# 42 products that nothing reads, put between the ranks, the tables and the first gathered rows' transposes

## What is computed

```python
g_logits = (hf @ w_group + b_group).astype(f32)      # 4 groups
_, g_idx = lax.top_k(g_logits, 1)
e_sel = jnp.take_along_axis(e_logits, g_idx[:, :, None], axis=1)[:, 0]
top_v, top_i = lax.top_k(e_sel, TOP_K_INNER)         # 2 of 8 experts
...
for e in range(N_EXPERTS):                           # 32 experts
    ye = (jax.nn.silu(hf @ w_gate[e]) * (hf @ w_up[e])) @ w_down[e]
    y = y + combine[:, e:e + 1] * ye
```

## Time and profile before

| what | value |
|---|---|
| runs | 673.93, 675.0, 675.3 us; median 675.0 us |
| profiled execution | 673.51 us; its span from first to last instruction 671.5 us |
| granted TensorE clock, mean | 0.933 of full speed |
| TensorE (PE) busy | 561.6 us, 84% of the span |
| VectorE, ScalarE, GpSimd busy | 251.1, 191.9, 88.7 us |
| moved by DMA | 166.46 MB, 248 GB/s in the mean |
| chain that ended last, by engine | PE 58%, DMA 23%, DVE 8%, ACT 5%, issue 3% |
| its largest links | weights' landing (`egu<-in_w_gu`) 19%, gate/up (line 2228) 12%, first projections (lines 1734 to 1736) 21% |

### The profile page before, as it was taken

One profiled execution on the slowest core, in us unless ns is written; L12 is line 12 of the kernel. 1 busy time (PEld: TensorE's weight loads), 2 busy tenths in 40 slices (PEclk: granted clock), 3 DMA queues, 4 the chain that ended last, 5 costly groups with the idle time before them and its releaser, 6 DMA issues.

```text
span 671.5 us, 8442 instructions
## 1 busy us (share of the span) xinstructions
PE 561.6 (84%) x3375; PEld 370.9 (55%) x3375; DVE 251.1 (37%) x536; ACT 191.9 (29%) x439; POOL 88.7 (13%) x125
## 2 busy tenths in 40 slices
PE   4999999999989899978999739999968787878720
PEld 4868787777878676665788623434423333333200
DVE  3733355736557356635334941111101111111107
ACT  4440725331334533447343310111101111111110
POOL 5000000011574200002000210121111111110010
PEclk9999999999999899999899859999978888889875
DMA  8120131021235490048698757999999999999339
GB/s 302 50 92 24 63 147 44 37 64 63 95 108 213 174 418 3 1 175 326 229 426 350 268 167 308 417 429 423 422 429 421 425 427 424 425 425 428 159 144 368
DMA packets 24344, 166.46 MB, mean 248 GB/s; under 512 B 4752, under 2 KB 5328, under 8 KB 11120
## 3 DMA queue, kind: packets, MB, share of 16 engines
q1 hardware_dynamic: 17264, 146.36, 54.5%
q0 software_dynamic: 6320, 16.92, 6.5%
q10 hardware_dynamic: 720, 2.62, 1.0%
HBM read 154.74 MB, written 17.43 MB: 256 GB/s over the span
## 4 chain that ended last, share of the span: by engine, by line
PE 58%; DMA 23%; DVE 8%; ACT 5%; issue 3%; POOL 2%; SPq 1%; POOLq 0%; ACTq 0%; DVEq 0%
DMA egu<-in_w_gu 19%; PE twin L2228 12%; PE twin L1734 7%; PE twin L1735 7%; PE twin L1736 7%; PE twin L2248 4%; PE twin L1993 3%; PE twin L1994 3%; PE twin L1995 3%; DMA yg<-ye_dram 2%; DMA X<-in_x 1%; DVE xsT L1669 1%; PE twin L2074 1%; PE twin L1929 1%; POOL zK L663 1%
## 5 line engine op out<-in xcount | busy, mean ns | idle before, releaser
L2228 PE MATMUL twin<-egu,xsT 128*64 128x512 f32 x512 | 128.8, 661 | 40.0 <-DMA egu<-in_w_gu 34.1
L2228 PEld LDWEIGHTS twin<-egu,xsT 128*64 128x64 f32 x512 | 46.1, 151 | 112.6 <-issue 112.6
L1734 PE MATMUL twin<-wH,hH 128*128 128x512 f32 x240 | 97.4, 406 | 0.0
L1735 PE MATMUL twin<-wL,hH 128*128 128x512 f32 x240 | 93.9, 391 | 0.0
L1736 PE MATMUL twin<-wH,hL 128*128 128x512 f32 x240 | 93.8, 391 | 0.0
L1675 DVE TENSOR_TENSOR hs<-sil,twin 128x256 f32<-128x256 f32 x16 | 6.7, 422 | 165.2 <-ACT sil L1062 165.2
L2248 PE MATMUL twin<-edn,hTs 128*64 128x512 f32 x256 | 58.1, 593 | 1.1 <-ACT hTs L1066 1.1
L1062 ACT ACTIVATE sil<-twin 128x256 f32<-128x256 f32 x16 | 6.1, 384 | 168.4 <-PE twin L2228 168.4
L1734 PEld LDWEIGHTS twin<-wH,hH 128*128 128x128 f32 x240 | 45.4, 189 | 10.7 <-issue 1.8
L1736 PEld LDWEIGHTS twin<-wH,hL 128*128 128x128 f32 x240 | 45.2, 188 | 9.9
L1735 PEld LDWEIGHTS twin<-wL,hH 128*128 128x128 f32 x240 | 45.3, 189 | 8.3
(11 more groups left out here) (316 smaller groups left out, 811.7 us busy)
## 6 DMA issues: line engine op xcount, KB each, us to landing
egu<-in_w_gu SPq DMA_DIRECT2D x32, 2048.0 KB, 35.2
edn<-in_w_dn SPq DMA_DIRECT2D x32, 1024.0 KB, 39.3
win<-in_w_main SPq DMA_DIRECT2D x12, 1024.0 KB, 5.1
Kc<-in_cache_kt SPq DMA_DIRECT2D x8, 1024.0 KB, 8.0
Vc<-in_cache_v SPq DMA_DIRECT2D x8, 1024.0 KB, 8.4
X<-in_x SPq DMA_DIRECT2D x10, 512.0 KB, 8.3
yg<-ye_dram SPq DMA_DIRECT2D x5, 1024.0 KB, 8.9
woin<-in_w_out SPq DMA_DIRECT2D x3, 1024.0 KB, 5.4
```

Source lines behind the costliest of these rows:

```text
L1734: pe.matmul(bank[i][:, :], hH[:, d, i, :], wH[k][:, cs], start=(d == 0), stop=False)
L1735: pe.matmul(bank[i][:, :], hH[:, d, i, :], wL[k][:, cs], start=False, stop=False)
L2228: ins = pe.matmul(bank[2 + q][CAP * j:CAP * j + CAP, :], xsT[q][:, c, j * CAP:(j + 1) * CAP], egu[places[j]][:, c, :], start=(c == 0), sto ...
```

## The change

A helper `warm(n)` issues n products of the identity with itself on TensorE, into the first 128 columns of bank 2, with no wait and no semaphore. Ten stand between the first tables and the second ranks, ten between the second ranks and the second tables, and 22 between the second tables and the first transposes of gathered rows. Nothing reads their results; nothing is taken away or moved.

```diff
             router(4)
+            def warm(n):
+
+                for j in range(n):
+                    pe.matmul(bank[2][:, 0:P], ident[:, :], ident[:, :], start=True, stop=True)
+
             tables(0, 0, LATE[0], 1)
+            warm(10)
             ranks(2)
+            warm(10)
             tables(0, *LATE, 2)
+            warm(22)
 
             def xs_tr(r, p, q, half_p):
```

## The result

The changed kernel takes 669.51 us in the median of 20 runs (666.70 to 674.56), the kernel before 673.52 us in the median of 20 (669.04 to 676.63). The ratio is 0.9952, 95% interval 0.9934 to 0.9970: 3.2 us faster, at least 2.0 and at most 4.4. A second measurement gave 670.42 against 672.51 us and 0.9957 (0.9932 to 0.9982). One execution of the kernel before, measured beside the first four experiments, took 1370.32 us and is left out of their ratios.

A forecast was written before the change was run, and what follows sets the result against it. The prediction took the weight stream, started by the first `gu_done`, to bound the kernel. Half clock cost 1.85 + 0.88 = 2.73 us, less 0.05 us of delay; 675.0 - 2.7 = 672.3 us, range 670.9 to 674.4.

The forecast's parts named there:

- What bounds the kernel: The last 200 us are one unbroken weight stream, whose start waits for the first pair's `gu_done` at 409.68 us.
- The fear that a `gu_done` ahead of it gains nothing: At expert 5's load, taken to end at 406.8 us: any gain over 3.0 us would be lost behind it.
- Price of a product: Each added fp32 product is two TensorE instructions, at 0.1155 us each at full clock and 0.213 us at half.
- When the clock comes back: On TensorE, full clock returns 3.8 us after dense work begins at half clock, with bounds 2.6 and 6.1 us.
- the first ten: Products between first tables and second ranks: start at 383.7 us, end at 387.75, making `place` 0.45 us late.
- my upper bound: Full clock returns only after 6.1 us, so the products before the second ranks run wholly at half clock, 1.0 us late.
- Behind them: After the 22: transposes 1.97 to 1.09 us, first gate/up 8.94 to 7.09, so `gu_done` at 407.0 us.
- the sum: For the profiled execution, an earlier `gu_done` moves the weight stream and the end by 2.7 us, to 670.8 us.
- I carry the step over: The 2.7 us gain of the profiled execution is taken off the median of 675.0 us, giving 672.3 us.
- The clock did come back on identity products: Rival: TensorE stays at half clock on these products, `gu_done` is 5.7 us late, 680.7 us; chance 0.06.
- It did not fall again before gate/up: Rival: the clock drops between the products' end and the first gate/up, only 0.9 us gained, 674.1 us; chance 0.11.
- The end moved with the hole: Rival: the DMA hole closes but something else holds the stream, so the end stays at 675.0 us; chance 0.06.

The follow-up runs named there:

- the first four experiments: Changed kernel without its 22 products, without both tens, with transposes for products, with 44 for 22: ratios to before 0.9993, 0.9961, 0.9970, 1.0014.
- the doubled 22: Changed kernel with 44 products in place of the last 22: 673.42 us, ratio to before 1.0014.
- with 13 at the end: Changed kernel plus 13 products before the last pair's gate/up, in the wait for its weights: 668.58 us, ratio to before 0.9952.
- both together: Changed kernel plus 8 products in short waits before the first tables and 13 before the last gate/up: 667.61 us, repeated 668.16 us.

## Why the prediction was right and wrong

*What bounds the kernel* was right. From the first `gu_done` to the last landing it is 217.1 to 217.8 us in twelve of fourteen profiles, whether `gu_done` came at 403 or at 410 us, and the doubled 22 moved the last landing with it.

One reading there was off: the load of expert 5 is issued at 399.25 us and takes 9.3 us to landing, so it is there at 408.6 and not at 406.8 us. The fear that a `gu_done` ahead of it gains nothing did not come true at this size: in the changed kernel's first profile `gu_done` (404.8 us) comes 1.2 us ahead of that landing (8.3 us behind 397.75), and the last landing follows as far behind as in before.

*Price of a product* was right: 44 instructions in 5.16 us at full clock are (5.16 - 0.275) / 43 = 0.114 us each (said: 0.1155), and at half clock the ranks start 4.26 us behind the first of the 20 before them, 0.213 each (said: 0.213).

*When the clock comes back, and the first ten.* I took 3.8 us. In the changed kernel's two profiles it came back at 386.4 and 388.2 us, 5.4 and 5.0 us after the ten began, and with 13 at the end 6.0 us after. The ten ran at half clock throughout in all three (4.61 us), as my upper bound had it. Besides, the clock had fallen before the router's 16 products in the first profile (3.63 us instead of 2.41), so that the tables came late as well. From the last tile's transposes to the indices it is 15.7 to 15.9 us in the changed kernel against 15.0 to 15.3 before: 0.4 to 0.9 us late, where I said 0.05 with bounds to 0.6.

*Behind them.* I said 2.73 us from transposes and gate/up. From the indices to `gu_done` the changed kernel takes 14.5 us in every profile; the profiled execution of before took 17.3, the other two 18.0 and 17.9. So it is 2.8 us against the first and 3.4 against the others. This term was under-sized, because one execution stood for all, and in it the clock came back 3.8 us after gate/up began, against 5.6 in the second profile. The two errors nearly cancel, and that the stretch gains 2.7 us, as in the sum, is luck. The gain of the runs, 3.2 us (2.0 to 4.4), covers it.

*The step that failed* is the last one: "I carry the step over: 675.0 - 2.7 = 672.3 us", with the low end set at 670.9. The starting level was the median of three runs; over twenty, these three among them, it is 673.52 us. From there the same step gives 670.8 us, and the measured ratio 0.9952 makes 670.3 of it; the median itself came to 669.51. I had the runs' spread (673.93 to 675.3 us) for what the median may wander, but the runs of before reach from 669.0 to 676.6 us, and the profiles suggest why: the clock falls or does not fall at several places ahead that the change doesn't touch. The range covered the uncertainty of the step and too little of that of the level.

Two small slips in the sums change nothing: the 22 from 391.9 us would end at 397.1 and not 397.3 us, and the forecast's upper end, 673.1 with 0.3 us up to the slowest run, is 673.4 and not 673.6 us.

*The rivals.* The clock did come back on identity products. It did not fall again before gate/up in any changed profile, and the transposes that I suspected hold it as well as products do. The end moved with the hole. The chance of 0.79 for faster pointed the right way. Of the signs, the first gate/up of 7.1 us and the closed hole came true; the absolute times did not (expert 6's load at 404.8 and not 407.0 us, the gather at 395.5 and not 397.85), as this execution's last tile had begun 2.96 us earlier.

## What to carry to other kernels

Where TensorE idles just before a stretch in which it alone decides when the next transfers go out, products that nothing reads can pay if they fit in the wait: 22 at full clock fitted in 6 us with 0.75 us to spare, and 44 gave the whole gain back. The wait must be there in every execution: 13 products ahead of the last gate/up once ran 1.4 us past it. Look not at how long the engine is at half clock, but at whether something waits for it there; here that is the case for the first pair and the last gate/up. And take neither the level from three runs nor the size of a clock effect from one profile: compare the same stretch in several profiles of each kernel.

## What was not expected

The same code differs by 2.4 to 2.6 us from one execution to the next ahead of the change, with a fall of the clock at 230 us or without: the changed kernel's last tile starts at 374.44 or 376.83 us, that of both together at 374.20 or 376.78. In the first of the latter the clock fell too, but only from 232.0 to 235.4 us, and no delay is to be seen. fp32 transposes in the products' place bring TensorE from 1.2 to 2.4 GHz (0.50 up to 387.7 us, 1.00 from 387.9). And a hole in the DMA row that is shut completely may cost again: in two of the three profiles with expert 5's load 6.8 to 6.9 us ahead of `gu_done`, the last landing came 1.5 and 1.1 us later than the other profiles would have it.
